# mLSTM gates: weights as the stationary tile, row-wise gate arithmetic with scans, and a spread to all partitions by DMA through DRAM

## What is computed

```
gates = h @ w_in[:, last 16 columns] + gate_b      # (256, 16): i_pre of 8 heads, f_pre of 8 heads
log_f = log_sigmoid(f_pre)
b     = cumsum(log_f)                              # over the positions
a     = i_pre - b
m     = b + running max(a, 0)                      # stabiliser
decay[t, s] = exp(a[s] - (m[t] - b[t])) for s <= t, else 0
scores = (q @ k.T) * scale * decay                 # per head
h = (scores @ v) / max(|row sum of scores|, exp(-m))
```

## Time and profile before

| | |
|---|---|
| median of 3 runs | 1605.41 us (1605.05 to 1606.14) |
| profiled execution | span 1608.2 us; the page gives no other time for it |
| PE busy | 1503.2 us (93%) |
| DVE busy | 1084.1 us (67%) |
| ACT busy | 748.4 us (47%) |
| DMA | 360.30 MB, mean 224 GB/s |
| mean granted PE clock | 0.963 |

### The profile page before, as it was taken

How to read it: one execution, slowest core, us unless ns; L and a number is a source line. 1 busy time by engine, 2 the same in 40 slices (tenths; PEclk the granted TensorE clock), 3 DMA queues, 4 the chain that set the end, 5 groups by cost and what they waited for, 6 DMA issues and landing times.

```text
span 1608.2 us, 21531 instructions
## 1 busy us (share of the span) xinstructions
PE 1503.2 (93%) x7461; PEld 1264.6 (79%) x7461; DVE 1084.1 (67%) x1317; ACT 748.4 (47%) x1078; POOL 36.7 (2%) x77
## 2 busy tenths in 40 slices
PE   1577999999999996999999999999999999999998
PEld 1455788888888875967988988988888889889886
DVE  5876588879789876558556646647647547547557
ACT  3223654544535547234444454454444444554552
POOL 1000100000000000000000000000000000000000
PEclk9977999999999997779999999999999999999999
DMA  8998589788888962649656666656656656656653
GB/s 313 355 313 291 148 300 328 275 303 310 298 271 324 328 224 100 235 168 327 182 172 186 190 172 184 189 172 187 187 173 187 183 179 186 183 178 187 183 176 113
DMA packets 196437, 360.30 MB, mean 224 GB/s; under 512 B 13240, under 2 KB 46344, under 8 KB 196124
## 3 DMA queue, kind: packets, MB, share of 16 engines
q1 hardware_dynamic: 196384, 359.61, 69.7%
HBM read 357.47 MB, written 2.10 MB: 224 GB/s over the span
## 4 chain that ended last, share of the span: by engine, by line
PE 81%; DVE 8%; DMA 5%; ACT 3%; issue 2%; SPq 0%; DVEq 0%; POOL 0%; ACTq 0%; POOLq 0%
PE proj L1092 24%; PE proj L1093 24%; PE proj L1094 24%; DVE ada_acc L699 4%; DMA ada_raw<-in_ada_w 3%; DVE w_lo L679 1%; PE mix L1176 1%; DMA raw<-in_att_w_in 1%; ACT w_hi L440 1%; PE mix L1299 1%; PE mix L1237 1%; ACT work L492 1%; DMA ada_raw<-in_x 1%; PE mix L1208 0%; PE mix L1194 0%
## 5 line engine op out<-in xcount | busy, mean ns | idle before, releaser
L679 DVE TENSOR_TENSOR w_lo<-raw,w_hi 128x1024 fp32r<-128x1024 f32 x480 | 586.3, 1223 | 432.2 <-ACT w_hi L440 427.9
L440 ACT ACTIVATE w_hi<-raw 128x1024 fp32r<-128x1024 f32 x480 | 508.2, 1063 | 739.2 <-PE proj L1094 684.0
L1092 PE MATMUL proj<-w_hi,h_hi 128*128 128x512 f32 x1312 | 528.7, 403 | 8.8 <-DVE h_lo L731 7.8
L1093 PE MATMUL proj<-w_lo,h_hi 128*128 128x512 f32 x1312 | 517.4, 394 | 0.0
L1094 PE MATMUL proj<-w_hi,h_lo 128*128 128x512 f32 x1312 | 517.3, 394 | 0.0
L1092 PEld LDWEIGHTS proj<-w_hi,h_hi 128*128 128x128 f32 x1312 | 250.7, 191 | 66.0 <-DVE h_lo L731 9.4
L1093 PEld LDWEIGHTS proj<-w_lo,h_hi 128*128 128x128 f32 x1312 | 250.8, 191 | 54.3 <-issue 3.3
L1094 PEld LDWEIGHTS proj<-w_hi,h_lo 128*128 128x128 f32 x1312 | 250.2, 191 | 53.5
L699 DVE SCALAR_TENSOR_TENSOR ada_acc<-ada_raw,cond,ada_acc 128x1024 f32<-128x1024 f32 x180 | 230.3, 1280 | 12.4 <-DMA ada_raw<-in_ada_w 9.6
L1092 PE MATMUL proj<-h_hi,w_hi 128*128 128x256 f32 x512 | 146.4, 286 | 3.3 <-DVE h_lo L731 3.3
L1094 PE MATMUL proj<-h_hi,w_lo 128*128 128x256 f32 x512 | 145.4, 284 | 0.0
(11 more groups left out here) (187 smaller groups left out, 1022.5 us busy)
## 6 DMA issues: line engine op xcount, KB each, us to landing
raw<-in_mlstm_w_in SPq DMA_DIRECT2D x256, 512.0 KB, 3.8
ada_raw<-in_ada_w SPq DMA_DIRECT2D x192, 512.0 KB, 6.2
raw<-in_att_w_in SPq DMA_DIRECT2D x128, 512.0 KB, 6.7
raw<-in_mlstm_w_out SPq DMA_DIRECT2D x64, 512.0 KB, 4.0
raw<-in_att_w_out SPq DMA_DIRECT2D x32, 512.0 KB, 6.2
stream<-in_x SPq DMA_DIRECT2D x1, 2048.0 KB, 8.5
ada_raw<-in_x SPq DMA_DIRECT2D x4, 512.0 KB, 7.7
out<-stream SPq DMA_DIRECT2D x4, 512.0 KB, 2.7
```

The costliest lines, as they stand in the source:

```text
L440: act.activation(w_hi[:, c % LEAD, :], raw[:, c % LEAD, :], ACT.Copy).then_inc(hi_ready, 1)
L679: dve.tensor_tensor(w_lo[:, c % LEAD, :], raw[:, c % LEAD, :], w_hi[:, c % LEAD, :].bitcast(F32), ALU.subtract).then_inc(lo_ready, 1)
L1092: pe.matmul(out_, a_hi, b_hi, start=start, stop=False, **kw)
L1093: pe.matmul(out_, a_hi, b_lo, start=False, stop=False, **kw)
```

## The change

- The gate weights become the stationary tile and h (256 positions) the moving one. The high and low parts are laid out 24 columns apart in a zeroed buffer, so that one stationary tile of 88 columns puts the input gates on PSUM rows 0 to 7 and the forget gates on rows 64 to 71: 16 x 3 matmuls, behind g4.
- The gate arithmetic is on rows of 8 x 256: ACT adds the bias while it evicts, the cumulative sum is a scan on DVE.
- `a` is stored to DRAM by a DMA that ACT issues, and read back from there with a partition step of zero into `a_bc` on all 128 partitions, by a second one. DVE adds the causal mask, and PE's broadcasts and ACT's copies of them go away.
- `turn_m` stands behind g7, the first scores wait no longer for the broadcasts, `decay1` waits for the mask.
- Two buffers more are zeroed on GpSimd (POOL) at the start, the gate bias is loaded by two DMAs, and the split of the gate weights is four instructions on ACT and on DVE.

```diff
+GATE_STEP, F_ROW = 24, 64
+GATE_M = F_ROW + H1
+GATE_W = GATE_STEP * (KT - 1) + GATE_M
...
-            sp.dma_start(gate_b[:], mlstm_gate_b[0:1, :].to_broadcast([P, 2 * H1])).then_inc(gates_in, 16)
+            for i, row in enumerate((0, F_ROW)):
+                sp.dma_start(gate_b[row:row + H1, :], mlstm_gate_b[0, i * H1:(i + 1) * H1].rearrange("(h o) -> h o", o=1)
+                             ).then_inc(gates_in, 16)
...
-            act.activation(gate_hi[:], gate_w[:], ACT.Copy).then_inc(gate_hi_ready, 1)
+            act.wait_ge(gate_zeroed, 2)
+            for i in range(2):
+                for hi_part, w in zip(gate_part(gate_hi, i), gate_raw(i)):
+                    op = act.activation(hi_part, w, ACT.Copy)
+            op.then_inc(gate_hi_ready, 1)
...
-                {8: [lambda: gates_exp(act)], 9: [lambda: gates_ln(act)],
-                 11: [lambda: floor_exp(act), lambda: bc_evac(act, (0, 1, 2))],
-                 12: [lambda: bc_evac(act, (3, 4, 5))], 13: [lambda: bc_evac(act, (6, 7))]},
+                {5: [lambda: gates_evac(act), lambda: gates_log(act)], 6: [lambda: a_store(act)],
+                 7: [lambda: a_spread(act)], 8: [lambda: floor_exp(act)]},
...
+        def gate_part(g, i):
+            first = i * F_ROW
+            most = g[:, first:first + GATE_STEP * (KT - 1)].rearrange("p (t g) -> p t g", g=GATE_STEP)
+            return most[:, :, 0:H1], g[:, first + GATE_STEP * (KT - 1):first + GATE_STEP * (KT - 1) + H1]
+        def gate_raw(i):
+            return gate_w[:, 0:KT - 1, i * H1:(i + 1) * H1], gate_w[:, KT - 1, i * H1:(i + 1) * H1]
+        def gates_evac(act):
+            act.wait_ge(gates_done, 1)
+            act.activation(f_row, mix[0][F_ROW:F_ROW + H1, 0:SEQ], ACT.Identity, bias=gate_b[F_ROW:F_ROW + H1, :])
+            act.activation(i_row, mix[0][0:H1, 0:SEQ], ACT.Identity, bias=gate_b[0:H1, :]).then_inc(g_act, 1)
+        def gates_log(act):
+            act.wait_ge(g_step, 1)
+            act.activation(e_row, e_row, ACT.Exp).then_inc(g_act, 1)
+            act.wait_ge(g_act, 2)
+            act.activation(e_row, e_row, ACT.Ln, bias=ones[0:H1, 0:1]).then_inc(g_act, 1)
+        def a_store(act):
+            act.wait_ge(row_step, 3)
+            act.dma_start(a_dram, a_row).then_inc(a_stored, 16)
+        def a_spread(act):
+            act.wait_ge(a_stored, 16)
+            act.dma_start(a_bc[:, :, P:3 * P], a_dram.rearrange("(o h) n -> o h n", o=1).to_broadcast([P, H1, SEQ])
+                          ).then_inc(a_in, 16)
...
         def gates_a(dve):
             dve.wait_ge(g_act, 1)
+            dve.scalar_tensor_tensor(out=e_row, in0=f_row, scalar=-1.0, in1=f_row, op0=ALU.mult, op1=ALU.min
+                                     ).then_inc(g_step, 1)
         def gates_rows(dve):
+            dve.wait_ge(g_act, 3)
+            dve.scalar_tensor_tensor(out=log_f, in0=f_row, scalar=0.0, in1=e_row, op0=ALU.min, op1=ALU.subtract
+                                     ).then_inc(row_step, 1)
             dve.wait_ge(row_step, 1)
+            dve.tensor_tensor_scan(out=cum_f, data0=log_f, data1=log_f, initial=0.0, op0=ALU.add, op1=ALU.min
+                                   ).then_inc(row_step, 1)
             dve.wait_ge(row_step, 2)
+            dve.tensor_tensor(a_row, i_row, cum_f, ALU.subtract).then_inc(row_step, 1)
+            dve.wait_ge(row_step, 3)
             dve.tensor_tensor_scan(out=m_row, data0=a_row, data1=a_row, initial=0.0, op0=ALU.max, op1=ALU.max
                                    ).then_inc(row_step, 1)
+            dve.wait_ge(row_step, 4)
             dve.tensor_tensor(m_tot, cum_f, m_row, ALU.add).then_inc(row_step, 1)
+        def bc_mask(dve):
+            dve.wait_ge(a_in, 16)
+            below = const[:, C_MASK:C_MASK + P].rearrange("p (o n) -> p o n", o=1).to_broadcast([P, H1, P])
+            dve.tensor_tensor(a_bc[:, :, 0:P], a_bc[:, :, P:2 * P], below, ALU.add)
+            dve.tensor_tensor(a_bc[:, :, 2 * P:3 * P], a_bc[:, :, 2 * P:3 * P], below, ALU.add).then_inc(bc_masked, 1)
...
-                {7: [lambda: gates_a(dve)], 8: [lambda: gates_b(dve)], 9: [lambda: gates_c(dve)],
-                 10: [lambda: gates_rows(dve)]},
+                {5: [lambda: gates_a(dve)], 6: [lambda: gates_rows(dve)], 9: [lambda: bc_mask(dve)]},
...
+            pool.memset(gate_hi[:].bitcast(F32), 0.0).then_inc(gate_zeroed, 1)
+            pool.memset(gate_lo[:].bitcast(F32), 0.0).then_inc(gate_zeroed, 1)
...
-            for t in range(NT):
-                for kt in range(KT):
-                    op = three(pe, mix[t][:, 0:2 * H1], h_hi[:, kt, t * P:(t + 1) * P], h_lo[:, kt, t * P:(t + 1) * P],
-                               gate_hi[:, kt, :], gate_lo[:, kt, :], kt == 0, kt == KT - 1)
+            for kt in range(KT):
+                w = slice(kt * GATE_STEP, kt * GATE_STEP + GATE_M)
+                op = three(pe, mix[0][0:GATE_M, 0:SEQ], gate_hi[:, w], gate_lo[:, w], h_hi[:, kt, :], h_lo[:, kt, :],
+                           kt == 0, kt == KT - 1)
...
             if isinstance(h, int) and h == 0:
-                pe.wait_ge(bc_ready, H1)
+                pe.wait_ge(g_act, 1)
...
-                {7: [lambda: gates1(pe)], 10: [lambda: gates_cum(pe)],
-                 11: [lambda: turn_m(pe), lambda: broadcast_a(pe, (0, 1, 2), 0)],
-                 12: [lambda: broadcast_a(pe, (3, 4, 5), 3)], 13: [lambda: broadcast_a(pe, (6, 7), 6)]},
+                {4: [lambda: gates1(pe)], 7: [lambda: turn_m(pe)]},
```

More of the change, by code:

```diff
@@ L161, in build @@
         qk_pad = part(9728, 4 * (SEQ + 3), "p (j t) -> p j t", j=4)
-        g_pre = part(2048, 32, "p (t g) -> p t g", t=NT)
-        g_a = part(2080, 16, "p (t g) -> p t g", t=NT)
-        g_b = part(2096, 16, "p (t g) -> p t g", t=NT)
-        log_f = part(2112, 16, "p (t g) -> p t g", t=NT)
+        i_row = work[0:H1, 2048:2304]
+        f_row = work[0:H1, 2304:2560]
+        e_row = work[0:H1, 2560:2816]
+        log_f = work[0:H1, 2816:3072]
         cum_f = work[0:H1, 3072:3328]
@@ L237, in build @@
             "y_hi_ready", "y_lo_ready", "gate_hi_ready", "gate_lo_ready"))
-        gates_done, g_step, g_act, cum_done = (sem(n) for n in (
-            "gates_done", "g_step", "g_act", "cum_done"))
-        row_step, bc_done, bc_ready, m_done = (sem(n) for n in (
-            "row_step", "bc_done", "bc_ready", "m_done"))
+        gates_done, g_step, g_act, gate_zeroed = (sem(n) for n in (
+            "gates_done", "g_step", "g_act", "gate_zeroed"))
+        row_step, a_stored, a_in, bc_masked = (sem(n) for n in (
+            "row_step", "a_stored", "a_in", "bc_masked"))
+        m_done, mask_step = (sem(n) for n in ("m_done", "mask_step"))
         neg_m_ready, floor_ready, conv_step, qk1_ready = (sem(n) for n in (
@@ L583, in squares1 @@
             op.then_inc(sq1_ready, 1)
-        def bc_evac(act, heads):
-            for h in heads:
-                act.wait_ge(bc_done, h + 1)
-                act.activation(a_bc[:, h, :], mix[BC_BANK[h % 3]][:, 0:3 * P], ACT.Copy).then_inc(bc_ready, 1)
         def act_group1(act, h, it, base):
@@ L899, in y1_out @@
             op.then_inc(y_done, 1)
-        def gates_exp(act):
-            act.wait_ge(g_step, 3)
-            act.activation(g_b, g_a, ACT.Exp).then_inc(g_act, 1)
-        def gates_ln(act):
-            act.wait_ge(g_step, 4)
-            act.activation(g_a, g_b, ACT.Ln).then_inc(g_act, 1)
+        def gate_part(g, i):
[20 more added lines that the diff above has]
+                          ).then_inc(a_in, 16)
         def floor_exp(act):
@@ L989, in dve_program @@
             dve.wait_ge(gate_hi_ready, 1)
-            dve.tensor_tensor(gate_lo[:], gate_w[:], gate_hi[:].bitcast(F32), ALU.subtract).then_inc(gate_lo_ready, 1)
+            for i in range(2):
+                for lo_part, hi_part, w in zip(gate_part(gate_lo, i), gate_part(gate_hi, i), gate_raw(i)):
+                    op = dve.tensor_tensor(lo_part, w, hi_part.bitcast(F32), ALU.subtract)
+            op.then_inc(gate_lo_ready, 1)
             dve.wait_ge(stream_zeroed, 1)
@@ L1252, in gates1 @@
             pe.wait_ge(gate_lo_ready, 1)
-            for t in range(NT):
-                for kt in range(KT):
-                    op = three(pe, mix[t][:, 0:2 * H1], h_hi[:, kt, t * P:(t + 1) * P], h_lo[:, kt, t * P:(t + 1) * P],
-                               gate_hi[:, kt, :], gate_lo[:, kt, :], kt == 0, kt == KT - 1)
+            for kt in range(KT):
+                w = slice(kt * GATE_STEP, kt * GATE_STEP + GATE_M)
+                op = three(pe, mix[0][0:GATE_M, 0:SEQ], gate_hi[:, w], gate_lo[:, w], h_hi[:, kt, :], h_lo[:, kt, :],
+                           kt == 0, kt == KT - 1)
             op.then_inc(gates_done, 1)
-        def gates_cum(pe):
-            pe.wait_ge(g_step, 6)
-            pe.matmul(mix[0][0:H1, 0:SEQ], log_f[:, 0, :], tri[:, 0:SEQ], start=True, stop=False,
-                      skip_group_check=True)
```

(17 more changed lines are left out.)

32 lines of the change are left out of this document (7 added, 25 removed).

## The result

| | median of runs | ratio to before | forecast |
|---|---|---|---|
| before, in the same comparison | 1605.78 us (1605.05 to 1609.44) | | |
| after | 1583.09 us (1582.27 to 1586.27) | 0.9846, 95% interval 0.9831 to 0.9861 | 1579.9 (1571 to 1589) |
| after, compared once more | 1584.14 us (1582.32 to 1589.14), before 1608.36 | 0.9863, 0.9837 to 0.9888 | |

The kernel is faster by 24.7 us (0.0154 x 1605.78) in the first comparison and by 22.0 in the second, about 1.5%; the forecast was 25.5. The profiled execution took 1586.27 us, with a span of 1584.5.

The account below looks back on a forecast made before the run. It took TensorE (PE, 81% of the chain) as the bound, idle or slow-clocked between g4 and g16. That stretch's terms summed to 51.5 against 77.0 us, 25.5 less, giving a median of 1579.9 us (1571 to 1589).

Parts of the forecast that it names:

- g5 to g7: Three of the first mLSTM head's weight granules (g0 to g31), right behind the new gate matmuls: 8.7 us.
- stretch: From the end of weight granule g4 to the start of g16 in head 0: 51.5 us against 77.0.
- the dense price: Gate matmuls cost as much as granule matmuls of the same moving size: 0.121 us each, 5.8 for 48.
- the lower bound: Gate matmuls at a cost in proportion to stationary width, 88/128: 4.0 us.
- The rival of a low clock in the gates: Gate matmuls run at low clock despite 256 columns: 10.2 instead of 5.8 us, g5 slower by 2.4, total 1586.7; chance 0.05.
- The first wait: PE idles 4.9 us at the turns behind g7, for a 10.7 us chain through ACT and DVE; g8 then 5.1.
- The second wait: PE idles 4.1 us at the first scores behind g14, for DVE's work and ACT's SiLU; g15 then 5.0.
- the late semaphore: Small store of the rows to DRAM: its completion signal could come surprisingly late; left open, 3 us taken.
- the outer bound of 8.5: Longest time allowed for the 1 MB spread from DRAM, taken from the 2 MB input load: 8.5 us.
- The cost of 0: Store and spread by DMA stay hidden, in near when DVE wants the mask: cost 0, at most 4 more.
- the rival in which the transfers fall behind: Spread late by 4 us and traffic after g16 short of 307 GB/s: 4 to 10 us more, 1584 to 1590; chance 0.18.
- The likeliest case: The sum with both of its waits holds: 1578 to 1582.5 us, chance 0.47; own range 1576 to 1584.

Follow-up runs that it names:

- the kernel with a wait of 1.0: Kernel after, with DVE adding the causal mask in step 12, behind the last convolution tap, instead of step 9: 1579.34 us, ratio 0.9829.
- the run with filled waits: Kernel after, with dense matmuls of unused result ahead of both PE waits, 40 at the turns and 30 at the scores: 1581.75 us, ratio 0.9834.
- the one with two more hops: Kernel after, with the 8 KB copied twice more inside DRAM between store and spread, ACT waiting for each: 1590.41 us, ratio 0.9893.

## Why the prediction was right, point by point

| step | forecast | measured |
|---|---|---|
| gate matmuls | 5.8 | 5.65 at clock 1.00 |
| g5 to g7 | 8.7 | 8.79 |
| wait and turns | 4.9 + 0.5 | 5.35 |
| g8 | 5.1 | 5.29 at 0.50 |
| g9 to g14 | 16.3 | 16.63 |
| wait at the scores | 4.1 | 3.59 |
| scores | 1.1 | 1.77 at 0.69 |
| g15 | 5.0 | 4.02 at 0.71 |
| stretch | 51.5 | 51.09 |
| g16 to the end of head 0 | 43.3 | 43.35 |

The sum is better than its terms: the scores came out 0.7 too long and g15 1.0 too short, and these cancel for the most part.

**The gates** cost what 48 matmuls of 256 moving columns cost at full clock: 0.118 us each, against 0.12 for the granules' matmuls with 128 columns in the stationary tile. The list of changes and the prediction gave the stationary tile 88 columns; it has 72 (64 + 8), as the timeline's row shows by its form. The sum took the dense price and is not touched by it, but the lower bound was worked out for the wrong width, and a cost in proportion to the width did not come about.

```profile
647.26 0.28 PE L1129 MATMUL mix<-h_hi,gate_hi 128*72 128x256 f32 x1
```

The rival of a low clock in the gates is refuted by the 1.00.

**The first wait** was right in its mechanism and its chain. The Exp began 0.01 us after its load had ended (658.10 + 1.28, 659.39), and Ln 0.01 after the second. The Trainium skill's drain of 1.38 us at each switch (ScalarE: Activation LUTs, What ACT_TABLE_LOAD costs) appears at neither, and with two of them the wait would have been 7.7 us instead of 4.83.

**The second wait** was right in its releaser and its bound; moving the mask took 2.5 us off it for 2.3 us of DVE work. It was 0.5 shorter than forecast. Behind it the clock did fall, but not at once: the scores at 0.69 and g15 at 0.71, 5.8 us together against a forecast of 6.1. In the second profile of the kernel they took 7.1 behind a wait of 3.7, so this term is good to about 1 us only. In the kernel with a wait of 1.0 the clock held.

**The transfers.** The store released ACT 2.8 us after its issue began (665.35 to 668.13; the forecast took 3), so the late semaphore that the prediction left open does not show here. The section of the Trainium skill that it cites for that, in DMA: Bandwidth & Descriptors, is written for DMAs that GpSimd issues; both DMAs here are ACT's. The spread took 9.0 us, above the outer bound of 8.5 that the prediction set, but 7.6, inside it, in the second profile of the same kernel. It was in some 1.1 us before DVE wanted it. The cost of 0 was right by that margin only, and the run with filled waits paid 2.2. What the variants show, and the prediction lacked, is how both times go with the other traffic. In the three kernels with the gates behind g3 the DMA engines were idle while the store was under way (a share of 0.02), and ACT got past it in 1.3 us without a wait; in the others that have it the share was 0.62 to 0.66 and it took 2.8 to 3.1. The spread took 5.1 to 5.4 us at a share of 0.65 to 0.80 (those three, and the one with two more hops) and 6.2 to 9.5 us at 0.88 to 0.95 (the five others), where SP had issued two adaLN tiles just ahead of it and a granule behind. No run varied the traffic alone. The traffic after g16 moved 334 GB/s at a share of 0.97 and delayed nothing; the rival in which the transfers fall behind is refuted for this kernel.

**What the prediction had wrong, without paying for it.** It booked 20.2 us on the broadcasts by matmul and the slow parts of three granules. Put back into the new kernel they cost 5.6 us, since all of it runs at full clock there and replaces a wait. The sum was right, since the old stretch was read as a whole, but the reason was not the number of matmuls. Nearly half of the old cost (28.33 - 19.20 = 9.1 us) was low clock, by the one profile in which they ran at full clock. It also called ACT's queue free up to some 10 us behind the store: 8.5 us more cost 6.2. And it charged the clock behind each wait as if it could be had alone; of g8's 2.6 us the run with filled waits got 0.3, because DVE then waits for the spread and the scores for DVE.

**The rest.** The likeliest case held, and the median was 3.2 us above its number. That is no term of the sum: the stretch saved 25.9, 0.4 more than forecast. In ratio to the runs of before beside it the gain was 24.7 and 22.0 us, and the intervals (22.3 to 27.1, and 18.0 to 26.2) hold the 25.5. In the profile the difference is the start of g0, 2.3 us later in after than in before, within a spread of 6.1 between executions. What sets this spread I did not test. In the two profiles with the latest g0 (628.78 and 628.02) the load of the input took 9.7 and 9.9 us and in the eleven others 8.4 to 9.2, so it can account for 1.5 of the 6.1 us at most.

## What to carry to other kernels

Before costing a removed operation, look at the clock it ran at: here nearly half of what eight small broadcasts cost was low clock, and one profile had them at full clock. Why is only in part shown. A wait taken from TensorE comes back at the next join if another engine has no slack up to it, so count that engine's work to the join and move tasks behind it; one entry in a table took 3.9 us off the stretch. A DMA round trip on an engine's own queue costs by what that engine feeds to others: two more hops held up ACT's weight copy, DVE behind it and PE behind that.
